# An encoder block on one Trainium2 core: a unit's row gathers start with block 0's first head, and block 1's taps, the taps of blocks 2-3 and the output gate are laid out anew beside them

## The chip, the core and the metric

The kernel runs on one core of one Trainium2 chip. The core's engines run side by side and meet at semaphores: TensorE (PE) multiplies matrices out of the on-chip memory into eight banks, VectorE (DVE) and ScalarE (ACT) work on tiles, GpSimd (POOL) issues the indirect gathers, SyncE (SP) the weight loads. 16 DMA engines carry all transfers. The metric is device time in microseconds (us), lower is better; everything is 32-bit.

## The reference

512 tokens of width 2048 go through a gated mixer and a layer of many small experts:

```python
proj = h @ w_in[l]
q, k, v, og, gkf, gkb, glu, ga, gb = jnp.split(proj, offsets, axis=-1)
...
o = (o * jax.nn.silu(og.reshape(B, S, GLA_HEADS, GLA_DV))).reshape(B, S, GLA_VAL_WIDTH)
y_a = o @ gla_w_o[l]
u = a_in * jax.nn.sigmoid(a_gate)
u = lax.conv_general_dilated(u, conv_w[l][:, None, :], ...)  # 31 taps, each channel alone
u = jax.nn.silu(_layernorm(u, conv_ln_g[l], conv_ln_b[l]))
y_b = u @ conv_w_pw2[l]
merged = jax.nn.sigmoid(ga) * y_a + jax.nn.sigmoid(gb) * y_b
x = x + merged @ w_out[l]
...
# experts: 8 heads; per token and head 16 of 16384 rows, found by two searches among 128 keys
s = jnp.einsum('thcd,hcnd->thcn', q, keys)
s_top, i_top = lax.top_k(s, PEER_TOPK)
...
u = jnp.take(u_tab, idx, axis=0)
act = jax.nn.gelu(jnp.einsum('thkd,td->thk', u, hb))
w = (gate * act)
return jnp.einsum('thk,thkd->td', w, jnp.take(v_tab, idx, axis=0))
```

## The kernel before

The tokens lie in four blocks of 128. The attention part (four heads, all blocks) and block 0's own mixer come first. Then comes the expert layer, which needs a row of 8 KB from `u_tab` and one from `v_tab` for each token, head and choice: 32 **units** (block and head) of 16 **steps**, and in each step 128 rows of either table, 2.1 MB in all. Everything that blocks 1 to 3 still need of the mixer is laid beside the steps of blocks 0 and 1 (steps 0 to 255).

A step on DVE is `add_row` for the step two before (x2 += w * v row, L1311), then `dot` (the u row times the token, summed, L1301), then `beside(s)`, which holds the work of other blocks, and, from unit 7 on, a part of the next unit's search. POOL has two row slots for u and four for v, so it gathers the u row of step s+2 as soon as `dot` of step s is done. ACT makes `expert` (gelu and gate) of each step and then its own `beside(s)`. PE has no steps: it runs through its slabs in the order of the code and waits for banks that DVE or ACT must free, and for weights.

Weights come as **slabs** of 2 MB (256 columns). The ring `wring` has two slots, and SP loads slab n when slab n-2 has been used (`hold(sp, w_used, ...)` in `load`). `project` is one projection of 128 channels over a span of tokens (16 matmuls), `tiles` two of them in one bank.

Beside block 0's steps blocks 1 to 3 get, by the tables at the head of the file (numbers are steps):

- `TURN_AT`: eight turns. In each PE makes the two GLU slabs of two channel tiles over 384 tokens (`glu1`), DVE takes them (`glu1_take`) and then makes 31 taps for each tile over 384 tokens (`conv1`, L1338), spread over the turn's steps. `u_keep` carries the 15 columns at the border to block 0.
- in turns 0 to 3 also two slabs of the output gate each (`og1_scale`, 384 tokens), in turns 4 to 7 two pairs of gate A and W_o for block 1 (`ma1_merge`).
- behind them gate B's eight slabs (`mb1_gate`), the layer norm of the taps over 384 tokens (`ln1`), the pointwise projection (`mb1_merge` at `PW_AT`), the output projection (`RES1_AT`), the norm (`NORM1_AT`) and the eight query heads of block 1, one every second step from 105.
- from step 130 (`M2_AT`) gate A, gate B and the rest for blocks 2-3.

Before the first step, block 0's eight query heads are searched: `topk_parts(0, PH, PH, ...)` makes each head's halves and pairs as its scores come, and then the places, keys and softmax of all eight in one batch (2048 wide). After that, `idx_ready` lets POOL start.

A semaphore wait blocks everything behind it on its engine: this is how a matmul that comes late holds ACT or DVE, and so the gathers.

## Time and profile before

| | before |
|---|---|
| time, median of 3 runs | 4772.74 us (4771.23 to 4778.17) |
| the profiled execution | 4765.59 us, its span 4763.9 us |
| PE busy | 3783.1 us (79%) |
| DVE busy | 2743.7 us (58%) |
| ACT busy | 873.1 us (18%) |
| GpSimd busy | 1339.6 us (28%) |
| DMA | 1530.72 MB, mean 321 GB/s; 1073.81 MB of them gathers |
| first row product, of step 0 | 1303.89 us |
| row product of step 54 | 1798.38 us |
| row product of step 120 | 2379.74 us |
| mean granted TensorE clock | 0.926 |

The shares are means over stages with different limits, so the stretches of the unit loop have to be read one by one. A matmul over 384 columns is a different amount of work from one over 128, and the same line has both; go by the shapes.

### The profile page before, as it was taken

The page shows a single profiled execution, that of the slowest core. Times are in us where ns is not written, and L with a number is a line of the kernel's source. Part 1 is how long each engine was busy: PE and PEld are TensorE (multiplying, and loading weights), DVE is VectorE, ACT ScalarE, POOL GpSimd, SP SyncE. Part 2 cuts the span into 40 slices and gives each one's busy share as a digit, 9 for nine tenths or more (in the row PEclk, how much of TensorE's full clock was granted, in tenths as well). Part 3 has the DMA queues.
Part 4 walks back from the last instruction along what each step waited for, and adds up shares of the span by engine and source line. Part 5 has one row for each costly group of instructions (what it writes and reads, how often), then busy time and mean ns, then how long its engine had stood idle before and what let it go on. Part 6 is the DMA issues. An engine that isn't in the chain of part 4 may idle for free. (4 is left out here: it accounts for less than half of the span.)

```text
span 4763.9 us, 44159 instructions
## 1 busy us (share of the span) xinstructions
PE 3783.1 (79%) x15280; PEld 2399.6 (50%) x15280; DVE 2743.7 (58%) x3996; ACT 873.1 (18%) x2035; POOL 1339.6 (28%) x1038
## 2 busy tenths in 40 slices
PE   6999999999999999766679798510788876777776
PEld 3444469996755576762668685310334432223232
DVE  1332249000599987866677777778665565455444
ACT  1322220100111111241111111111111211212111
POOL 0000000000022221323454444455333333344443
PEclk9999999999999999888889899755899999999999
DMA  2111126677588888999999999999999999999998
GB/s 102 54 70 53 53 106 264 251 273 277 212 336 352 346 363 329 414 407 407 418 388 426 396 426 418 380 360 341 359 372 367 378 357 372 383 420 421 415 417 367
DMA packets 194520, 1530.72 MB, mean 321 GB/s; under 512 B 24279, under 2 KB 30551, under 8 KB 30809
## 3 DMA queue, kind: packets, MB, share of 16 engines
q0 software_dynamic: 147456, 1073.81, 56.3%
q1 hardware_dynamic: 45232, 444.87, 23.6%
q10 hardware_dynamic: 1740, 10.91, 0.6%
q8 instruction: 46, 0.75, 0.1%
q14 instruction: 46, 0.38, 0.0%
HBM read 1525.32 MB, written 4.19 MB: 321 GB/s over the span
## 5 line engine op out<-in xcount | busy, mean ns | idle before, releaser
L582 POOL DMA_INDIRECT arena_c<-in_peer_u,arena_c x384 | 539.4, 1405 | 2904.3 <-DVE arena_c L1301 1563.2
L1301 DVE SCALAR_TENSOR_TENSOR arena_c<-arena_c 128x2048 f32<-128x2048 f32 x384 | 878.8, 2289 | 590.8 <-DMA arena_c<-in_peer_u,arena_c 584.6
L1624 PE MATMUL bank<-arena_h,wring 128*128 128x384 f32 (+3 forms) x3200 | 887.9, 440 | 25.6 <-ACT arena_h L727 9.0
L586 POOL DMA_INDIRECT arena_c<-in_peer_v,arena_c x512 | 643.4, 1257 | 423.5 <-DVE arena_h L1528 171.7
L1728 PE MATMUL bank<-arena_h,wring 128*128 128x128 f32 (+2 forms) x4608 | 660.6, 305 | 100.0 <-DVE arena_h L1380 52.5
L1624 PEld LDWEIGHTS bank<-arena_h,wring 128*128 128x128 f32 x3200 | 542.8, 197 | 367.1 <-issue 160.3
L1728 PEld LDWEIGHTS bank<-arena_h,wring 128*128 128x128 f32 x4608 | 617.0, 193 | 146.1 <-issue 81.8
L1936 PE MATMUL bank<-arena_c,arena_h 128*128 128x512 f32 x1024 | 504.8, 641 | 170.9 <-ACT arena_h L886 150.6
L1970 PE MATMUL bank<-arena_c 128*128 128x512 f32 x1024 | 485.4, 623 | 173.2 <-ACT arena_c L930 162.7
L1311 DVE SCALAR_TENSOR_TENSOR arena_o<-arena_c,arena_o 128x2048 f32<-128x2048 f32 x256 | 600.7, 2346 | 7.1 <-ACT arena_c L765 4.6
L763 ACT ACTIVATE arena_c<-arena_c 128x1 f32<-128x1 f32 x384 | 77.9, 203 | 2206.1 <-DVE arena_c L1301 2206.0
L1528 DVE SCALAR_TENSOR_TENSOR arena_h<-arena_h,arena_c 128x2048 f32<-128x2048 f32 x128 | 292.8, 2292 | 298.1 <-DMA arena_h<-in_peer_u,arena_c 296.9
L1970 PEld LDWEIGHTS bank<-arena_c 128*128 128x128 f32 x1024 | 193.6, 197 | 465.0 <-ACT arena_c L930 246.4
L1936 PEld LDWEIGHTS bank<-arena_c,arena_h 128*128 128x128 f32 x1024 | 200.0, 204 | 446.6 <-issue 262.8
L1728 PE MATMUL bank<-arena_c,wring 128*128 128x128 f32 (+1 forms) x1536 | 238.6, 318 | 48.4 <-ACT arena_c L704 28.9
L1338 DVE SCALAR_TENSOR_TENSOR arena_c<-arena_c,cols 128x384 f32<-128x384 f32 x480 | 259.6, 608 | 0.0
L1728 PEld LDWEIGHTS bank<-arena_c,wring 128*128 128x128 f32 x1536 | 219.7, 198 | 67.3 <-issue 41.0
L1728 PE MATMUL bank<-arena_o,wring 128*128 128x128 f32 (+1 forms) x1536 | 236.9, 317 | 17.1 <-DMA wring<-in_gla_w_o 15.3
L1728 PEld LDWEIGHTS bank<-arena_o,wring 128*128 128x128 f32 x1536 | 217.9, 196 | 36.1 <-DMA wring<-in_gla_w_o 18.0
L1811 PE MATMUL bank<-arena_c 128*128 (+1 forms) x128 | 25.1, 339 | 261.3 <-ACT arena_c L734 258.7
L1649 PE MATMUL bank<-wring,arena_h 128*128 128x512 f32 x512 | 221.9, 594 | 0.3
L1786 PE MATMUL bank<-wring,arena_h 128*128 128x512 f32 x384 | 178.7, 624 | 39.1 <-DMA wring<-in_w_out 25.0
(214 smaller groups left out, 2558.8 us busy)
## 6 DMA issues: line engine op xcount, KB each, us to landing
wring<-in_w_in SPq DMA_DIRECT2D x112, 2048.0 KB, 8.2
wring<-in_gla_w_o SPq DMA_DIRECT2D x24, 2048.0 KB, 9.9
wring<-in_conv_w_pw SPq DMA_DIRECT2D x24, 2048.0 KB, 11.1
wring<-in_w_out SPq DMA_DIRECT2D x24, 2048.0 KB, 13.5
wring<-in_peer_w_q SPq DMA_DIRECT2D x24, 2048.0 KB, 11.0
arena_c<-in_peer_v,arena_c POOLq DMA_INDIRECT x512, 11.4
arena_c<-in_peer_u,arena_c POOLq DMA_INDIRECT x384, 8.4
arena_c<-in_x SPq DMA_DIRECT2D x4, 1024.0 KB, 12.6
```

Of the source, the lines that this page charges most:

```text
L582: pool.indirect_dma_start(out=u_rows[s], out_offset=None, in_=u_tab[0], in_offset=at)\
L586: pool.indirect_dma_start(out=v_rows[s], out_offset=None, in_=v_tab[0], in_offset=at)\
L1301: V.scalar_tensor_tensor(row, row, 1.0, block_of(h2, b), ALU.mult, ALU.mult, accum_out=act_u[:, k:k + 1]).then_inc(u_used, 1)
L1311: V.scalar_tensor_tensor(block_of(x2, b), by_tile(v_row[s]), act_w[:, k:k + 1], block_of(x2, b), ALU.mult, ALU.add).then_inc(v_used, 1)
L1338: ins = V.scalar_tensor_tensor(dst, upad1[:, m, r:r + T1], tap, dst, ALU.mult, ALU.add)
L1528: V.scalar_tensor_tensor(row, row, 1.0, block_of(h2, b), ALU.mult, ALU.mult, accum_out=act_u2[:, m, k:k + 1]).then_inc(u2_used, 1)
L1624: last = M(ps[bank][:, 0:hi - lo], w_slot(slot)[:, k, m * P:m * P + P], act_in[:, k, lo:hi], start=k == 0, stop=k == KT - 1)
L1649: last = M(by_half(ps[b][:]), hT[:, kk, b * P:b * P + P], w_slot_half(s)[:, :, k, :], start=kk == 0, stop=kk == KT - 1)
L1728: last = M(ps[bank][:, m * w:(m + 1) * w], w_slot(slot)[:, k, m * P:m * P + P], act_in[:, k, lo:hi], start=k == 0, stop=k == KT - 1)
L1786: last = M(by_half(ps[bank0 + g * nb + b][:]), lhs(kk, b), w_slot_half(s)[:, :, k, :], start=kk == 0, stop=kk == KT - 1)
L1936: last = M(ps[4 + q][:], diag1[:, k % VS, :], v_row[k % VS][:, q * 512:q * 512 + 512], start=k == 0, stop=k == TOP - 1)
L1970: last = M(ps[4 * m + q][:], diag[:, s, :], v2_row[s][:, q * 512:q * 512 + 512], start=k == 0, stop=k == TOP - 1)
```

## The change

It rearranges the work up to step 127; from step 128 on the order is the same.

- **Start.** Block 0's heads are searched one by one (`topk_0`). The index of head 0 is handed to POOL as soon as it is there; head 1 follows, and heads 2 to 7 are searched beside steps 0 to 5. ACT takes the queries of heads 4 to 7 beside steps 0 and 1.
- **Turns.** They start at step 8 and are 6 or 7 steps long. `glu1` makes the two GLU slabs over 384 tokens and one gate B slab over 128. DVE makes block 1's taps alone (128 columns). The GLU values of blocks 2-3 are put raw into `cv`, and the 15 border columns are kept.
- **Fill.** Blocks 2-3's taps (256 columns) are made from these by `fill`, 63 pieces for each of 8 pairs of tiles (one for two copies, 62 taps), spread by the table `FILL` over steps 53 to 104.
- **Output gate.** All eight slabs come behind the turns, one in three steps from 58; PE starts them only when ACT has taken all of gate B (`pair["mb1"]["sig"]`).
- **Norms.** Block 1 (128 columns) at steps 62 to 68, blocks 2-3 (256 columns, `ln2`) at 115 to 131; PE makes the latter's sums between the queries and the slabs of blocks 2-3.
- **Then** gate A with W_o, one pair in each of steps 81 to 88; the pointwise merges two a step from 91; residuals at 96, 97, 99, 100; block 1's queries one a step from 105.
- Buffers move to make room, and some semaphores are merged (`cv_done`, `mg_done`, `passed`, `out1`).

```diff
-TURN_AT = (0, 10, 20, 30, 40, 47, 54, 61, 68)
-OG_AT = (4, 7)
-IT_AT = (2, 4)
...
+TURN_AT = (8, 15, 21, 28, 34, 41, 47, 54, 60)
+GB_LATER = 3
+OG_AT = tuple(range(58, 82, 3))
+XC1_AT, RSTD1_AT, RECIP1_AT, SCALE1_AT = 62, 65, 66, 67
+IT_AT = tuple(range(81, 89))
...
+FILL = ((53, 0), (78, 70), (86, 250), (95, 420), (104, 8 * 63))
+XC2_AT, RSTD2_AT, RECIP2_AT, SCALE2_AT = 115, 121, 122, 123
...
+            for h in range(2):
+                queries0(h)
+                exponentials(h, 1, work_0)
+            queries0(2)
+            queries0(3)
...
+                if s == 0:
+                    queries0(4)
+                    exponentials(2, 1, work_0)
+                    queries0(5)
+                if s == 1:
+                    queries0(6)
+                    exponentials(3, 1, work_0)
+                    queries0(7)
+                if 2 <= s < 6:
+                    exponentials(s + 2, 1, work_0)
...
-            find, softmax = topk_parts(0, PH, PH, lambda c, b: s_0[:, c, b, :], work_0, lambda a: a[:, 0:PH, :])
-            all_of(find)
-            softmax()
...
+                    chain.mark(V.tensor_tensor(upad1[:, m, PAD:PAD + GL], ps[2 + m][:, 0:GL], sig1[:, m, 0:GL], ALU.mult))
+                    V.tensor_tensor(cv[:, 2 * j + m, 2 * P:T], ps[2 + m][:, P:T1], sig1[:, m, P:T1], ALU.mult)\
                         .then_inc(p["use"], 1)
...
+                if s < PH - 2:
+                    find, softmax = topk_0(s + 2)
+                    all_of(find)
+                    softmax()
...
-                if 0 <= s - QUERY1_AT < 2 * PH and (s - QUERY1_AT) % 2 == 0:
-                    h = (s - QUERY1_AT) // 2
+                if 0 <= s - QUERY1_AT < PH:
+                    h = s - QUERY1_AT
...
+            for h in range(2):
+                find, softmax = topk_0(h)
+                all_of(find)
+                if h == 0:
+                    V.tensor_copy(idx_cur[:, 0, :], idx_all[:, 0, :]).then_inc(idx_ready, 1)
+                softmax()
...
+                slab_ready(first + 2, i, per)
+                pe.wait_ge(pair["mb1"]["sig"], i * 2 + (m0 + 1))
+                tiles(slot, hT, 4 + m0, P, 2 * P, pair["mb1"]["gate"])
                 slab_used()
...
+            pe.wait_ge(pair["mb1"]["sig"], 2 + 8)
+            og1_slab(0)
+            og1_slab(1)
+            pe.wait_ge(pair["glu1"]["use"], 2 + KT)
+            pe.wait_ge(cv_done, 2 * KT)
+            ln_mean(ln1, P, 2 * P)
+            og1_slab(2)
+            for t in range(KT):
+                pe.wait_ge(ln1["sq"], t // 2 + 1)
+                M(ps[1][:, 0:P], ones_d[:], sqr1[:, t // 2 % 3, t % 2, :], start=t == 0, stop=t == KT - 1)\
+                    .then_inc(ln1["sq_used"], 1)
+            for n in range(3, 8):
+                og1_slab(n)
             pe.wait_ge(og1["used"], 4 + KT)
```

On DVE, between two row additions (L1311, L1313) beside gate A's merges. Before, step 44:

```order
L1311 SCALAR_TENSOR_TENSOR arena_o<-arena_c,arena_o 128x16x128
L1301 SCALAR_TENSOR_TENSOR arena_c<-arena_c 128x2048
L1357 TENSOR_TENSOR arena_h<-bank,arena_c 128x2x128
L1338 SCALAR_TENSOR_TENSOR arena_c<-arena_c,cols 128x384 x9
L1311 SCALAR_TENSOR_TENSOR arena_o<-arena_c,arena_o 128x16x128
```

The same engine in the changed program, step 82, which also holds a merge of gate A:

```order
L1313 SCALAR_TENSOR_TENSOR arena_o<-arena_c,arena_o 128x16x128
L1303 SCALAR_TENSOR_TENSOR arena_c<-arena_c 128x2048
L1376 TENSOR_TENSOR arena_h<-bank,arena_c 128x2x128
L1327 SCALAR_TENSOR_TENSOR arena_c<-arena_c,cols 128x256 x23
L1313 SCALAR_TENSOR_TENSOR arena_o<-arena_c,arena_o 128x16x128
```

The nine taps of 384 columns beside a merge have become 23 of 256 columns, and a merge now comes in every step.

On ACT, at the end of block 0's queries. Before, behind the loop over the heads (L745 is the exponential of all eight, L763 and L765 are step 0's expert):

```order
L745 ACT_TABLE_LOAD
L745 ACTIVATE arena_c<-arena_c 128x128
L772 ACT_TABLE_LOAD
L772 ACTIVATE arena_c<-bank0 128x384
L772 ACTIVATE arena_c<-bank1 128x384
L763 ACT_TABLE_LOAD
L763 ACTIVATE arena_c<-arena_c 128x1
L765 ACTIVATE arena_c<-arena_c,gate_all 128x1
```

In the changed program, from step 0's expert (L751, L753) over head 4's queries (L717) and scores (L722) to head 2's exponential (L728):

```order
L751 ACT_TABLE_LOAD
L751 ACTIVATE arena_c<-arena_c 128x1
L753 ACTIVATE arena_c<-arena_c,gate_all 128x1
L717 ACTIVATE arena_c<-bank0 128x128
L717 ACTIVATE arena_c<-bank1 128x128
L722 ACTIVATE arena_c<-bank2 128x128
L722 ACTIVATE arena_c<-bank3 128x128
L728 ACT_TABLE_LOAD
L728 ACTIVATE arena_c<-arena_c 128x16
```

Head 2's exponential now stands behind head 4's queries, which wait for PE.

On PE, behind block 1's last GLU slab. Before: gate A's last two pairs, gate B, and the norm's sums over 384 columns (L1884, L1889):

```order
L1728 MATMUL bank<-arena_h,wring 128x128 x32
L1728 MATMUL bank<-arena_o,wring 128x128 x32
L1728 MATMUL bank<-arena_h,wring 128x128 x32
L1728 MATMUL bank<-arena_o,wring 128x128 x32
L1728 MATMUL bank<-arena_h,wring 128x128 x128
L1884 MATMUL bank<-arena_c,ones_d 128x384 x16
L1889 MATMUL bank<-arena_c,ones_d 128x384 x4
```

In the changed program, between block 1's last query head and the slabs of blocks 2-3:

```order
L1859 MATMUL bank<-arena_c 128x128
L1955 REGISTER_ALU
L1955 COMPARE_AND_BRANCH
L1921 MATMUL bank<-arena_c,ones_d 128x256 x16
L1965 MATMUL bank<-arena_c,ones_d 128x256 x16
```

The sums over blocks 2-3 have moved from before the pointwise projection to behind the queries.

## Rows read from the trace of the kernel before

**Rows 1.** The page's 40 slices: busy tenths of the DMA engines.
```profile
DMA  2111126677588888999999999999999999999998
```
**Rows 2.** Stretches: length, busy us (x) of PE, PEld, DVE, ACT, POOL, PEclk, DMA share, GB/s.
```profile
2063.00:2147.00 84.00, 67.13 (x513) 65.64 (x514) 47.95 (x49) 28.18 (x45) 19.03 (x19) 0.89 1.00 411
2147.00:2233.00 86.00, 63.56 (x128) 26.01 (x126) 41.56 (x32) 11.79 (x26) 27.19 (x18) 0.88 1.01 422
2258.00:2375.00 117.00, 76.78 (x544) 74.82 (x544) 82.04 (x87) 14.99 (x64) 56.01 (x33) 0.82 1.00 415
1892.00:1973.00 81.00, 64.49 (x512) 63.03 (x512) 71.73 (x90) 20.09 (x33) 20.09 (x16) 0.89 0.97 398
1640.00:1980.00 340.00, 303.40 (x1731) 237.68 (x1730) 284.41 (x373) 65.14 (x116) 73.64 (x64) 0.96 0.90 363
1303.00:1640.00 337.00, 331.67 (x1017) 191.65 (x1016) 312.16 (x388) 57.12 (x122) 88.65 (x78) 1.00 0.89 345
...
885.00:1130.00 245.00, 230.70 (x1995) 224.91 (x1995) 9.35 (x22) 15.14 (x31) 0.00 (x0) 1.00 0.71 269
```
**Rows 3.** DVE's timeline, start and us: from the first scores to the first step.
```profile
1214.44 0.49 DVE L1190 MAX8 arena_c<-arena_c 128x8 f32<-128x128 f32 x2 [15.45 <-ACT arena_c L739]
...
1295.61 0.17 DVE L1455 COPY arena_c<-idx_all 128x16 uint32<-128x16 uint32 x1
1303.89 2.29 DVE L1301 SCALAR_TENSOR_TENSOR arena_c<-arena_c 128x2048 f32<-128x2048 f32 x1 [8.11 <-DMA arena_c<-in_peer_u,arena_c]
...
1314.74 0.56 DVE L1322 TENSOR_TENSOR arena_c<-bank,arena_c 128x384 f32<-128x384 f32 x1 [7.99 <-PE bank L1624]
```
**Rows 4.** DVE's timeline: a step without a wait, and block 0's taps.
```profile
1497.98 2.28 DVE L1301 SCALAR_TENSOR_TENSOR arena_c<-arena_c 128x2048 f32<-128x2048 f32 x1
...
1500.19 3.26 DVE L1338 SCALAR_TENSOR_TENSOR arena_c<-arena_c,cols 128x384 f32<-128x384 f32 x6
1503.37 2.34 DVE L1311 SCALAR_TENSOR_TENSOR arena_o<-arena_c,arena_o 128x2048 f32<-128x2048 f32 x1
1505.63 2.28 DVE L1301 SCALAR_TENSOR_TENSOR arena_c<-arena_c 128x2048 f32<-128x2048 f32 x1
...
799.71 12.43 DVE L1112 SCALAR_TENSOR_TENSOR arena_c<-arena_c,cols 128x128 f32 x47
```
**Rows 5.** DVE's timeline: the halves and the pairs of one head alone (unit 7).
```profile
2326.89 0.48 DVE L1190 MAX8 arena_c<-arena_c 128x8 f32<-128x128 f32 x2
...
2330.30 2.35 DVE L1311 SCALAR_TENSOR_TENSOR arena_o<-arena_c,arena_o 128x2048 f32<-128x2048 f32 x1
...
2336.72 0.42 DVE L1220 TENSOR_TENSOR arena_c<-arena_c 128x256 f32<-128x256 f32 x1
...
2339.68 2.35 DVE L1311 SCALAR_TENSOR_TENSOR arena_o<-arena_c,arena_o 128x2048 f32<-128x2048 f32 x1
```
**Rows 6.** PE's timeline: GLU pair, a pointwise slab, first query, first slab of blocks 2-3.
```profile
1272.79 41.92 PE L1624 MATMUL bank<-arena_h,wring 128*128 128x384 f32 x128 [0.46 <-ACT arena_c L739]
...
2063.80 9.18 PE L1728 MATMUL bank<-arena_c,wring 128*128 128x128 f32 x64 [28.95 <-ACT arena_c L704]
...
2073.33 7.38 PE L1728 MATMUL bank<-arena_c,wring 128*128 128x128 f32 x64 [0.36 <-issue]
...
2257.95 9.37 PE L1624 MATMUL bank<-arena_h,wring 128*128 128x128 f32 x64 [3.49 <-ACT arena_h L727]
...
2375.05 15.60 PE L1728 MATMUL bank<-arena_h,wring 128*128 128x256 f32 x64 [0.67 <-ACT arena_c L739]
```
**Rows 7.** DVE's timeline: the row products of steps 54 and 120.
```profile
1798.38 2.29 DVE L1301 SCALAR_TENSOR_TENSOR arena_c<-arena_c 128x2048 f32<-128x2048 f32 x1
...
2379.74 2.29 DVE L1301 SCALAR_TENSOR_TENSOR arena_c<-arena_c 128x2048 f32<-128x2048 f32 x1 [5.25 <-DMA arena_c<-in_peer_u,arena_c]
```
**Rows 8.** Weight loads of 1303 to 1640, then of 1990 to 2400: median us to landing.
```profile
wring<-in_w_in SPq DMA_DIRECT2D x16, 2048.0 KB, 10.8
...
wring<-in_w_out SPq DMA_DIRECT2D x8, 2048.0 KB, 13.8
```

More of the change, by code:

```diff
@@ L60 @@
 SB_GLU1 = SB_WQ0 + PH
[L61 to L65 removed]
+SB_OG1 = SB_GLU1 + 24
+SB_MA1 = SB_OG1 + 8
+SB_PW1 = SB_MA1 + 16
 SB_OUT1 = SB_PW1 + 8
@@ L1312, in add_row, with taps @@
                                        ALU.mult, ALU.add).then_inc(v_used, 1)
+            def taps(j, first, end, src, lo, hi, done):
+                for n in range(first, end):
+                    r, m = n // 2, n % 2
+                    dst = cv[:, 2 * j + m, lo:hi]
+                    tap = cols[:, 2 * j + m, R_CW + r:R_CW + r + 1]
+                    if r == 0:
+                        ins = V.tensor_scalar(dst, src[:, m, 0:hi - lo], tap, cols[:, 2 * j + m, R_CB:R_CB + 1],
+                                              ALU.mult, ALU.add)
+                    else:
+                        chain.wait(but=1)
+                        ins = V.scalar_tensor_tensor(dst, src[:, m, r:r + hi - lo], tap, dst, ALU.mult, ALU.add)
+                    if r < TAPS - 1:
+                        chain.mark(ins)
+                    else:
+                        ins.then_inc(done, 1)
+                        chain.wait()
             def glu1_take(j):
@@ L1398, in beside @@
+                if s in OG_AT:
+                    og1_scale(OG_AT.index(s))
+                if s == XC1_AT:
                     dve.wait_ge(ln1["sum"], 1)
-                    dve.wait_ge(cv1_done, KT)
-                    mean = ps[0][:, 0:T1].unsqueeze(1).broadcast_to([P, 2, T1])
-                    for g in range(2 * (s - XC_AT), 2 * (s - XC_AT) + 2):
-                        dst = cv[:, 2 * g:2 * g + 2, P:T]
-                        V.tensor_tensor(dst, dst, mean, ALU.subtract).then_inc(ln1["xc"], 1)
@@ new lines, in beside @@
+                if s <= FILL[-1][0]:
+                    fill(filled(s - 1), filled(s))
+                if 0 <= s - XC2_AT < 4:
+                    dve.wait_ge(ln2["sum"], 1)
+                    dve.wait_ge(cv_done, 3 * KT)
+                    mean = ps[0][:, 0:T2].unsqueeze(1).broadcast_to([P, 2, T2])
+                    for g in range(2 * (s - XC2_AT), 2 * (s - XC2_AT) + 2):
+                        dst = cv[:, 2 * g:2 * g + 2, 2 * P:T]
+                        V.tensor_tensor(dst, dst, mean, ALU.subtract).then_inc(ln2["xc"], 1)
@@ L1829, in _, with glu1 @@
             pe.wait_ge(s_ev, 2 * PH)
-            def glu1(first, i, per, before, j):
+            def glu1(first, i, per, m0):
                 p = pair["glu1"]
+                slot = first % 2
                 slab_ready(first, i, per)
                 for m in range(2):
-                    pe.wait_ge(p["use"], j * 2 + (2 * before + m + 1))
-                    project(0, m, hT, m, p["gate"], P, T)
+                    pe.wait_ge(p["use"], i * 4 + (2 * m0 + m + 1))
+                    project(slot, m, hT, m, p["gate"], P, T)
                 slab_used()
@@ L1852, in ma1 @@
                 slab_used()
[L1854 to L1862 removed]
+            with pe.Fori(0, PH // 2) as i:
+                for m in range(2):
+                    glu1(SB_GLU1 + 3 * m, i, 6, m)
@@ new lines, in og1_slab, with ln_mean @@
+            def og1_slab(n):
+                slab_ready(SB_OG1 + n)
+                for m in range(2):
+                    pe.wait_ge(og1["used"], 2 * n + m + 1)
+                    project(n % 2, m, hT, 4 + 2 * (n % 2) + m, og1["mm"], P, T)
+                slab_used()
+            def ln_mean(ln, lo, hi):
+                for t in range(KT):
+                    last = M(ps[0][:, 0:hi - lo], ones_d[:], cv[:, t, lo:hi], start=t == 0, stop=t == KT - 1)
+                last.then_inc(ln["sum"], 1)
@@ L1863, in _ @@
             pe.wait_ge(og1["used"], 4 + KT)
[L1864 removed]
+            with pe.Fori(0, PH // 2) as i:
                 for a in range(2):
[L1866 to L1876 removed]
@@ L1878, in _ @@
-            pe.wait_ge(pair["ma1"]["use"], 2 + 8)
-            for n in range(4):
-                mb1_gate(n)
-            pe.wait_ge(pair["glu1"]["use"], 2 + KT)
-            pe.wait_ge(cv1_done, KT)
-            for t in range(KT):
-                last = M(ps[0][:, 0:T1], ones_d[:], cv[:, t, P:T], start=t == 0, stop=t == KT - 1)
-            last.then_inc(ln1["sum"], 1)
-            for n in range(4):
-                for t in range(4 * n, 4 * n + 4):
-                    pe.wait_ge(ln1["sq"], t + 1)
-                    M(ps[1][:, 0:T1], ones_d[:], sqr1[:, t % 2, :], start=t == 0, stop=t == KT - 1)\
-                        .then_inc(ln1["sq_used"], 1)
-                mb1_gate(4 + n)
+                    ma1(SB_MA1 + 2 * a, i, 4, a, i * 2 + (a + 1))
```

347 lines of the change are left out of this document (160 added, 187 removed).

## The prediction

> **What bounds the kernel now.** Start with the page's slices [rows 1]: from slice 17 (1906 us) on the 16 DMA engines are nine tenths busy or more, but for the last slice; in the five before, eight tenths. The stretches with their sums [rows 2] say what is busy instead. At 1303 to 1640 us TensorE (PE) is busy for 332 of 337 us and DVE for 312, the DMA moves 345 GB/s; at 1640 to 1980 it is 303 and 284 of 340 at 363 GB/s; from 2063 on it is DMA alone, 411 to 422 GB/s, with PE and DVE half idle. So two regimes stand one behind the other in the unit loop: first PE and DVE together, then DMA. All that the change touches lies between the first score (1214 us) and the first slab of blocks 2-3 (PE at 2375.05 us, just before the step of 2379.74 us) [rows 3, 6, 7]. Behind that point the program is the same, and the DMA is full, so what is gained or lost there is carried to the end one for one. I therefore follow PE and DVE to that point.
>
> **The prices.** A step's row product and row addition follow each other at 2.21 and 2.26 us, and six 384-wide taps between them take 3.18, so a step is 4.47 us and a tap 0.53 [rows 4]. 47 taps of 128 columns take 12.43 us, 0.264 each [rows 4]. A 256-wide tap is not in the trace: its bounds are 0.264 and 0.53, and the line through both gives 0.397, which I take. A split tap thus costs 0.264 + 0.397 - 0.53 = 0.13 us more, and 496 of them 65 us of DVE: both parts pay what does not depend on the columns. The Trainium skill (VectorE: DVE Perf Modes, on the TRN2 errata) speaks against such a split: each instruction pays its fixed latency, and it gives 58 cycles plus the columns at 0.96 GHz, while noting that this row is too low. By its row the split would cost an estimated 30 us in place of 65; the 128-wide row here is above it (0.264 against an estimated 0.19 us), so the trace decides.
> One head's search alone: halves 3.41 us (2326.89 to 2330.30), pairs 2.96 (2336.72 to 2339.68), six 256-wide ones for the keys at the 0.45 of such a row, 2.7, and ten small ones of 0.07 to 0.2 [rows 5], together 10.4 us.
> PE: a 384-wide slab (two projections) is 41.92 / 2 = 20.95 us, a 128-wide one 7.4 (7.38 in [rows 6]). The ring has two slots, so a slab's load starts when the slab two before it is used, and short slabs go at (7.4 + load) / 2 each (my reading of the code). Without gathers 32 of them take 245 us, 7.7 each; with gathers beside them eight took 81 us from 1892 and eight 84 us from 2063, 10.1 to 10.5 each [rows 2]. Load times are 10.8 us beside gathers and up to 13.8 for a half-slab at full DMA [rows 8].
>
> **The start.** Removed: the wait of 8.11 us for the first row and the batch's tail [rows 3]. Now: head 0's index is ready 10.3 us after its scores, at 1225, and the first row lands about 8.3 us later (1295.61 to 1303.89), at 1234. DVE has head 1 done at 1236 and makes dot 0. But beside steps 0 to 5 it makes six more searches: 8 x 4.47 + 6 x 10.4 = 98 us, and ScalarE stands between: it holds the queries of heads 4 to 7 in front of the exponentials, so steps 0 and 1 end only with PE's heads 4 and 6, about 15 us lost. Step 8, where block 1's first GLU pair is taken, comes at 1344. PE finished that pair at 1320 (its search phase ends 5 us later than before), and waits. Before, it was taken at 1315 in step 0 [rows 3]. So eight steps are won and 29 us of PE lost.
>
> **The turns (steps 8 to 54).** PE now makes two 384-wide slabs and one 128-wide one: 42 + 7.4. The next pair's first slab starts to load when the second long slab is used, so it comes after the load (10 us, by the row of 10.8) and not after 7.4: 52.3 a turn. DVE needs 6.5 steps x 4.47 + 62 x 0.264 + 1.9 for the take = 47.4. PE ends the turns: first two by DVE (to 1440), five by PE, last take at 1701. Before, step 54 was at 1798 [rows 7].
>
> **Output gate (steps 54 to 79).** PE may not start before ScalarE has taken the last B gate, three steps after the take (1731): 22 us idle. Then 8 slabs x 20.95, one mean and one square sum (4 and 5 us): 1910 at step 79. DVE needs some 5.8 us a step (4.47, 2.8 wide taps, a third of the gate's two products of 0.5) and PE gives 7, so DVE waits in step 58 (11 us), 62, 64 and then every third.
>
> **Gate A with W_o (steps 79 to 88).** 16 short slabs. DVE has 22.5 wide taps a step: 4.47 + 8.9 + 0.4 = 13.8. PE: with gathers at half their pace I take 8.7 a slab (bounds 7.7 and 10.1), 17.4 a pair, one pair a step: the ring ends it, last merge 2050.
>
> **Pointwise (88 to 94).** PE waits for the merges of step 91, DVE has 19 taps a step (12.0 us): last merge 2137, where before it was about 2146, just ahead of the projection [rows 2].
>
> **Output projection (to step 100).** Before 86 us [rows 2]; with fewer gathers beside it I take loads of 11.5 in place of 13.8 [rows 8]: 73, to 2211. Then one residual, three steps with nine taps each, the norm and the transposes: queries start at 2252 (before 2257.95, [rows 6]).
>
> **Queries.** Before 117 us for eight heads, 14.6 each, since a head went with two steps; now one step a head. At 4.2 MB per head and step and 415 to 422 GB/s: 10 us, less two slabs that are there: 77, to 2329.
>
> **Blocks 2-3's norm.** New on PE's path: mean (7 us), then the squares of steps 116 to 119, which wait for seven DVE steps of 5.5 to 6.5 us: PE starts blocks 2-3's slabs at 2374 in place of 2375, step 120 at 2377 in place of 2380.
>
> **Sum.** 41 us of the queries, 13 of the projection and the 97 us by which the steps had run ahead at step 54 are given back in gate A, in the taps beside it, and in 45 us of the new norm. Shift -1 to -3: the profiled execution's 4765.6 us would be 4763, and the median of the three timed runs, 7 us above it, 4770.
>
> **Rivals.** All three engines are near their ends here. DVE's own work from step 8 to 120 is 112 x 4.47 + 496 x 0.661 + some 67 of merges and norms = 896 us in my 1030, and DMA has 112 x 2.1 MB and 70 slabs of 2.1 MB, 382 MB, 371 GB/s.
> Faster: the loads are quick where the gathers pause at a take or a merge. With the 7.7 of the stretch without gathers: turns -15, gate A -15, projection -11, queries -11, about -50: 4720. For it speaks that DMA at 415 GB/s would need 920 us only, and DVE 896; against it the 10.8 of a stretch that was not full.
> Slower: the two-slot ring keeps the full pace's price of 10.1 a slab: gate A + 22, turns + 8, and PE partly at 1.2 GHz after each wait (9.18 us for a slab after 28.95 us idle, in place of 7.38 [rows 6], in a stretch of granted clock 0.89 [rows 2]) in the pointwise, query and norm parts, + 8: 4808. It decides from 9.3 us a slab on. For it speaks that each of these parts lies beside gathers.
> The DMA pages' limit. Rows show 422 GB/s over 86 us [rows 2]; the Trainium skill (DMA: Bandwidth & Descriptors, where 436 GB/s comes from) says that HBM to SBUF binds near 358 GB/s per core. Were it so, 382 MB would need an estimated 1067 us, + 37: 4807. The trace disagrees, 2 in 100.
> The change does not do what it says: the first searches beside steps 0 to 5 could run without ScalarE's hold, -11, or hold all six steps, + 25. This only moves the cases above.
>
> **How the numbers follow.** The sum holds within 20 us: 0.42, of it a third faster, half the same. Quick loads (4700 to 4750): 0.30. Slow ring (4785 to 4830): 0.26, the limit of HBM 0.02. The measurement tells 0.2%, 9.5 us, from no change: faster 0.43, same 0.24, slower 0.33. The range of 8 in 10, 4712 to 4815, takes in most of both rivals; the likeliest case alone has 4750 to 4790.
>
> **What would show it.** First gather near 1226 us; first take near 1344, with PE idle some 17 us before the next 384-wide slab; turns of 52 us with a gap of 2 to 3 us before each pair; a PE gap of 20 us before the first output-gate slab; short slabs in gate A at 8.7 us each; queries at 10 us a head; first 256-wide slab of blocks 2-3 at 2374. If the turns or the gate A pairs are off by more than 2 us each, or wide taps cost more than 0.42 us, the forecast falls.

## The result

The changed kernel takes 4810.26 us (median of 7 runs, 4795.67 to 4813.93), the kernel before 4778.98 beside it (7 runs, 4771.23 to 4791.29): a ratio of 1.0054, 95% interval 1.0036 to 1.0071. Measured again later it was 4808.08 against 4773.66 us, 1.0073 (1.0054 to 1.0092). It is slower by 25 to 35 us. The forecast was 4770 us, 3 us less than the 4772.74 of the kernel before that it started from, so the sign was missed; the time lies in the range, at the place of the rival "slow ring" (4808). The two executions that were profiled lie 45 us apart (4810.88 and 4765.59), the medians 31, so the two traces side by side show the loss some 14 us too large.

### The profile page after: what moved, and what is told of

It is laid out like the page before. It is cut to its first block and busy times, and to the rows that moved or that the text cites. A ratio compares the mean times of both kernels' runs of the same rounds, so it can differ in the third digit from the quotient of the medians.

```text
span 4809.1 us, 44984 instructions
## 1 busy us (share of the span) xinstructions
PE 3795.9 (79%) x15344; PEld 2409.2 (50%) x15344; DVE 2831.0 (59%) x4650; ACT 893.5 (19%) x2064; POOL 1473.1 (31%) x1038
## 5 line engine op out<-in xcount | busy, mean ns | idle before, releaser
L565 POOL DMA_INDIRECT arena_c<-in_peer_u,arena_c x384 | 518.6, 1350 | 2815.3 <-DVE arena_c L1303 1528.2
L1672 PE MATMUL bank<-arena_h,wring 128*128 128x384 f32 (+3 forms) x3200 | 896.4, 443 | 89.6 <-DMA wring<-in_w_in 20.9
L569 POOL DMA_INDIRECT arena_c<-in_peer_v,arena_c x512 | 800.4, 1563 | 424.1 <-DVE arena_h L1576 171.2
L1313 DVE SCALAR_TENSOR_TENSOR arena_o<-arena_c,arena_o 128x2048 f32<-128x2048 f32 x256 | 600.7, 2347 | 2.7
L751 ACT ACTIVATE arena_c<-arena_c 128x1 f32<-128x1 f32 x384 | 77.8, 203 | 2054.9 <-DVE arena_c L1303 2054.8
L1327 DVE SCALAR_TENSOR_TENSOR arena_c<-arena_c,cols 128x128 f32<-128x128 f32 (+1 forms) x960 | 324.6, 410 | 0.0
```

Source lines behind the costliest of these rows:

```text
L565: pool.indirect_dma_start(out=u_rows[s], out_offset=None, in_=u_tab[0], in_offset=at)\
L569: pool.indirect_dma_start(out=v_rows[s], out_offset=None, in_=v_tab[0], in_offset=at)\
L1313: V.scalar_tensor_tensor(block_of(x2, b), by_tile(v_row[s]), act_w[:, k:k + 1], block_of(x2, b), ALU.mult, ALU.add).then_inc(v_used, 1)
L1327: ins = V.scalar_tensor_tensor(dst, src[:, m, r:r + hi - lo], tap, dst, ALU.mult, ALU.add)
L1672: last = M(ps[bank][:, 0:hi - lo], w_slot(slot)[:, k, m * P:m * P + P], act_in[:, k, lo:hi], start=k == 0, stop=k == KT - 1)
```

## The profile after

**Where the time went.** The prediction said that all of the difference arises between the first scores and step 120, and is then carried on one for one. These are that stretch and all behind it, for the kernel before and then the changed one (length, busy us of PE, PEld, DVE, ACT, POOL, granted clock, DMA share, GB/s):

```profile
1199.00:2379.70 1180.70, 996.98 (x4911) 724.68 (x4912) 918.07 (x1211) 239.32 (x502) 317.82 (x244) 0.93 0.89 359
2379.70:4760.00 2380.30, 1684.83 (x4947) 944.89 (x4945) 1481.86 (x1880) 428.45 (x1201) 1019.35 (x780) 0.89 0.97 388
```
```profile
1206.00:2424.60 1218.60, 999.91 (x4955) 727.24 (x4956) 998.35 (x1858) 227.63 (x495) 456.34 (x243) 0.91 0.88 348
2424.60:4805.00 2380.40, 1691.59 (x4966) 949.63 (x4965) 1488.80 (x1891) 460.53 (x1237) 1014.41 (x782) 0.89 0.97 388
```

The second rows are 2380.30 and 2380.40 us long: behind step 120 nothing changed. Ahead of the stretch the changed kernel was 7 us later (1206 against 1199), in block 0's own mixer, whose slabs stand in the same order in both. That is not scatter alone: the first scores come at 1214.4 and 1215.2 us in the two traces that run the old code there (before and e5), and at 1217.9 to 1222.3 in all eleven of the changed kernel and its edits. At 885 us they are still together; from there to 1130 us PE was busy for 230.70 us before [rows 2], and after for

```profile
885.00:1130.00 245.00, 226.54 (x1943) 220.70 (x1943) 9.35 (x22) 15.13 (x31) 0.00 (x0) 0.99 0.70 261
```

(226.0 to 227.7 us in all eleven), with waits for the loads of w_in of 7.2 us in place of 2.0. So 3 to 8 us of the loss lie ahead of all that the forecast looked at; what in the change makes them was not tested. The stretch itself is 37.9 us longer (29.7 in the trace of c0, the changed kernel measured again). PE is busy for 3 us more, so nearly all of it is idle PE: 183.7 us before, 218.7 now. DVE's 80 us more stand beside that and needn't be its cause. And the transfers, which do the same work in both, fell from 359 to 348 GB/s.

**Which waits.** Groups of PE's instructions in the same stretch, the large ones (busy us, mean ns, idle time before them and what ended it), first of the kernel before:

```profile
L1624 PE MATMUL bank<-arena_h,wring 128*128 128x384 f32 (+1 forms) x2560 | 632.0, 410 | 15.3 <-issue 5.2 <-ACT arena_h L727 4.4 <-DMA wring<-in_w_in 4.3
L1728 PE MATMUL bank<-arena_h,wring 128*128 128x128 f32 (+1 forms) x1039 | 125.9, 283 | 17.3 <-DMA wring<-in_w_in 13.1 <-issue 2.9 <-ACT arena_c L739 0.7
L1728 PE MATMUL bank<-arena_c,wring 128*128 128x128 f32 x512 | 66.7, 297 | 43.2 <-ACT arena_c L704 28.9 <-DMA wring<-in_conv_w_pw 13.6 <-issue 0.7
L1728 PE MATMUL bank<-arena_o,wring 128*128 128x128 f32 x512 | 65.0, 293 | 14.7 <-DMA wring<-in_gla_w_o 14.5
L1811 PE MATMUL bank<-arena_c 128*128 x64 | 14.0, 352 | 42.6 <-ACT arena_c L734 42.6
L1580 PE MATMUL bank<-ident,arena_c 128*128 128x128 f32 x32 | 7.3, 424 | 25.0 <-DVE arena_c L1175 25.0
```
and of the changed one:
```profile
L1672 PE MATMUL bank<-arena_h,wring 128*128 128x384 f32 (+1 forms) x2560 | 639.7, 413 | 79.2 <-DMA wring<-in_w_in 20.9 <-ACT arena_c L777 20.4 <-DVE arena_c L1345 18.5
L1776 PE MATMUL bank<-arena_h,wring 128*128 128x128 f32 x1024 | 122.8, 282 | 16.7 <-DMA wring<-in_w_in 11.1 <-issue 2.7 <-DVE arena_h L1376 1.5
L1776 PE MATMUL bank<-arena_c,wring 128*128 128x128 f32 x512 | 65.1, 293 | 30.0 <-DVE arena_c L1387 22.6 <-DMA wring<-in_conv_w_pw 6.2 <-DVE arena_h L1376 0.8
L1776 PE MATMUL bank<-arena_o,wring 128*128 128x128 f32 x512 | 64.1, 290 | 14.0 <-DMA wring<-in_gla_w_o 13.9
L1965 PE MATMUL bank<-arena_c,ones_d 128*128 128x256 f32 x27 | 12.7, 642 | 23.0 <-ACT arena_c L829 23.0
L1859 PE MATMUL bank<-arena_c 128*128 x64 | 12.0, 313 | 8.6 <-ACT arena_c L717 8.6
L1628 PE MATMUL bank<-ident,arena_c 128*128 128x128 f32 x32 | 7.3, 424 | 34.9 <-DVE arena_c L1178 34.9
```

The 384-wide slabs, which hardly waited before (15.3 us), wait for 79.2 now: for loads in the turns (20.9), for ScalarE's last B gate ahead of the output gate (20.4), for DVE to reach step 8 (18.5). The scores wait 34 us less (42.6 to 8.6), since a head goes with one step; the pointwise slabs 13 less; blocks 2-3's squares wait 23.0 us and the norm's transposes 10 more. The short slabs of gates A and B and of W_o wait for their loads no longer than before: 27.6 us then (13.1 and 14.5), 25.0 now. So gate A's loads are a miss of the forecast, as shown below, and not what the change lost against the kernel before; that lies mostly in the long slabs.

**The parts.** The stretches of after that answer to [rows 2]: start, turns, output gate, gate A, pointwise, projection, queries, blocks 2-3's norm.

```profile
1226.00:1354.00 128.00, 102.47 (x628) 82.20 (x626) 108.44 (x335) 32.89 (x69) 22.84 (x20) 0.94 0.80 316
1354.00:1727.00 373.00, 347.63 (x1280) 217.57 (x1280) 332.06 (x623) 68.10 (x143) 240.89 (x95) 0.97 0.94 373
1755.00:1935.00 180.00, 175.92 (x576) 104.49 (x576) 142.23 (x178) 53.83 (x104) 82.49 (x43) 0.99 0.86 336
1936.00:2091.00 155.00, 127.62 (x1024) 124.59 (x1024) 121.65 (x236) 29.12 (x45) 19.47 (x20) 0.92 0.91 359
2091.00:2187.00 96.00, 65.08 (x512) 63.70 (x512) 79.05 (x153) 2.98 (x12) 11.76 (x12) 0.84 0.82 313
2187.00:2265.00 78.00, 62.57 (x128) 25.73 (x128) 62.10 (x107) 2.98 (x12) 12.94 (x12) 0.91 0.96 394
2299.00:2382.00 83.00, 69.39 (x544) 66.76 (x544) 48.09 (x51) 12.03 (x50) 31.83 (x19) 0.93 0.95 394
2382.00:2427.00 45.00, 21.86 (x65) 15.02 (x66) 40.24 (x50) 9.33 (x32) 16.33 (x12) 0.70 0.91 350
```

Only the output gate has one engine busy throughout (PE, 175.92 of 180 us). No part reaches the 411 to 422 GB/s that the kernel before had from 2063 us on [rows 2]. The page's slices, where [rows 1] had nine tenths from slice 17 on, show a break in it, in slice 18:

```profile
DMA  2111136677789989989999999998999999999998
```

**Steps.** Rows of DVE's timeline that answer to [rows 3] and [rows 7]: the first scores, the first row product, and those of steps 8, 54, 120 and 128.

```profile
1221.90 0.49 DVE L1193 MAX8 arena_c<-arena_c 128x8 f32<-128x128 f32 x2 [15.74 <-ACT arena_c L722]
...
1242.97 2.29 DVE L1303 SCALAR_TENSOR_TENSOR arena_c<-arena_c 128x2048 f32<-128x2048 f32 x1
...
1352.22 2.29 DVE L1303 SCALAR_TENSOR_TENSOR arena_c<-arena_c 128x2048 f32<-128x2048 f32 x1 [0.91 <-DMA arena_c<-in_peer_u,arena_c]
...
1719.32 2.29 DVE L1303 SCALAR_TENSOR_TENSOR arena_c<-arena_c 128x2048 f32<-128x2048 f32 x1 [1.25 <-DMA arena_c<-in_peer_u,arena_c]
...
2424.57 2.28 DVE L1303 SCALAR_TENSOR_TENSOR arena_c<-arena_c 128x2048 f32<-128x2048 f32 x1
...
2483.14 2.29 DVE L1303 SCALAR_TENSOR_TENSOR arena_c<-arena_c 128x2048 f32<-128x2048 f32 x1 [4.74 <-DMA arena_c<-in_peer_u,arena_c]
```

At step 54 the steps are 79 us ahead of before (1719.3 against 1798.4), at step 80, by the same rows, 103 (1946.7 against 2049.8); at step 88 it is 37, at step 96 they are 20 behind (2208.4 against 2188.6), at step 120 they are 45. So 123 us are lost in 16 steps: gate A and the pointwise part take two slabs to a step, 16.4 us a step, where before a step took 8.7.

## The experiments

The theories as the expectations name them. **R**, later **P**: a part ends with PE, the load of its next slab (two slots) and the engine that PE hands to; the time is the sum of that chain. **V**: DVE's added work is the loss. **S**: what counts of the early start is gathers made early. **G** came up after the first four runs: what counts is PE's chain and also how many steps lie beside it, since a step that doesn't fit there is made later at its full price. Every time has the kernel before beside it on its chip: 4779.68 us for the first four, 4773.66 for c0, e6, e7 and e9, 4781.62 for e5, e8 and e10. "Against the change" is by the ratios to before for the first four, by the medians of one set for the rest.

### e1_few_taps: blocks 2-3's taps left out

```diff
-                        taps(j, at - 1, at, upad2, 2 * P, T, cv_done)
+                        if at <= 2 or at > 60:
+                            taps(j, at - 1, at, upad2, 2 * P, T, cv_done)
```


> The changed kernel with 56 pieces of each 62 taps of blocks 2-3 left out (its output for them is another one), 464 wide taps of 0.397 us, 184 us of DVE, in steps 53 to 104. Theory R (from step 8 on PE and the load of its next slab end each part, DVE waits): gate A's 16 slabs stay at 150 to 155 us, the pointwise part loses PE's wait of 21 us, the rest little, so 25 to 45 us less than the changed kernel (profiled 4809). Theory V (DVE's added work, 65 us of split taps and 62 us of searches beside steps, sets the time): DVE's parts shrink by its work, 100 us or more less, gate A's part under 125 us.

4779.44 us (8 runs), ratio 0.9997 (0.9985 to 1.0009): 27 to 36 us less than the change (by its first and second ratio), within R's bounds, far from V's. That is as much as the whole loss: without 184 us of DVE's taps the kernel is level with the one before. Gate A beside it:

```profile
1925.00:2080.00 155.00, 132.26 (x1031) 128.10 (x1029) 52.25 (x58) 30.32 (x46) 23.76 (x21) 0.91 0.92 366
```

DVE is busy for 52.25 us in place of 121.65, and the part is as long: 1928.43 to 2079.6, 151 us against 155. Its 16 slabs, not DVE, end it. The gain came mostly behind it, where PE waits for DVE: the third pointwise slab waited 7.99 us, not 21.16, the norm's transposes 17.7, not 27.8. V falls for gate A and stands for these places.

### e2_gate_banks: the first output-gate slab into free banks

PE need not wait for ScalarE's last B gate before that slab. The banks change in the programs of ScalarE and DVE too.
```diff
-                    project(n % 2, m, hT, 4 + 2 * (n % 2) + m, og1["mm"], P, T)
+                    project(n % 2, m, hT, 6 - 2 * (n % 2) + m, og1["mm"], P, T)
...
-            pe.wait_ge(pair["mb1"]["sig"], 2 + 8)
             og1_slab(0)
+            pe.wait_ge(pair["mb1"]["sig"], 2 + 8)
             og1_slab(1)
```


> The changed kernel, but the output gate's first slab goes to the banks that gate B does not use, so PE need not wait for ScalarE's last gate B: PE's gap of 20.4 us before the output gate should go. Theory R: PE is what later parts wait for, so 12 to 20 us less than the changed kernel (about 1.001 to 1.003 of the kernel before in place of 1.0054). Theory V: the steps do not move, 0 to 5 us.

4790.77 us (10 runs), ratio 1.0025 (1.0014 to 1.0036): 14 to 23 us less than the change. The wait of 20.43 us is now 3.16, for a load, and the slab starts 18 us earlier:

```profile
1736.95 22.60 PE L1672 MATMUL bank<-arena_h,wring 128*128 128x384 f32 x64 [3.16 <-DMA wring<-in_w_in]
```

A handover of 20 us that the forecast had right was simply a cost of the change, and it could be had without.

### e3_half_loads: half of each slab in gate A not loaded

```diff
-            pair_loads(SB_MA1, w_in, WGA, w_o, 0)
+            with sp.Fori(0, KT // 2) as i:
+                load(SB_MA1, i, 2, slot_all(0)[:, 0:SLAB // 2], slab(w_in, i + WGA)[:, 0:SLAB // 2])
+                load(SB_MA1 + 1, i, 2, slot_all(1)[:, 0:SLAB // 2], slab(w_o, i)[:, 0:SLAB // 2])
```


> The changed kernel, but each of the 16 slabs of block 1's gate A and W_o loads only its first half (the other half of the slot is what was there, so block 1's values are others). Theory R (the two-slot ring's load sets 9.7 us a slab there): the part from 1936 to 2091, 155 us, falls to 120 to 130, and the whole by 20 to 30 us. Theory V: DVE's 13.9 us a step set that part, it stays above 145 and the whole within 8 us.

4781.57 us (10 runs), ratio 1.0009 (1.0000 to 1.0019): 21 to 31 us less. The part and two of its slabs, then two of the same part in the changed kernel:

```profile
1925.00:2052.00 127.00, 118.69 (x1025) 115.54 (x1024) 122.12 (x237) 30.33 (x46) 20.52 (x21) 1.00 0.80 300
1943.39 7.41 PE L1778 MATMUL bank<-arena_h,wring 128*128 128x128 f32 x64 [0.50 <-issue]
1951.25 7.41 PE L1778 MATMUL bank<-arena_o,wring 128*128 128x128 f32 x64 [0.46 <-DMA wring<-in_gla_w_o]
```
```profile
1957.35 10.03 PE L1776 MATMUL bank<-arena_h,wring 128*128 128x128 f32 x64 [5.32 <-DMA wring<-in_w_in]
...
2042.71 10.02 PE L1776 MATMUL bank<-arena_o,wring 128*128 128x128 f32 x64 [4.56 <-DMA wring<-in_gla_w_o]
```

155 us became 127, 7.9 a slab, with all of DVE's work in place (122.12 of it). This shows the load as what ends gate A, in two ways: the wait of up to 5 us, and a slab that takes 10.03 us in place of 7.41 behind such a wait, at a granted clock of 0.92 in the part against 1.00 without waits. The second is 9 of the 28 us (127.62 less 118.69).

### e4_late_start: all eight heads searched before the first gather

```diff
-            for h in range(2):
+            for h in range(8):
```
This stands in DVE's and in ScalarE's program, and the searches beside steps 0 to 5 go. ScalarE then makes a head's exponential behind the next head's queries, and head 0's index is handed over last.

> The changed kernel with its early start undone: all eight heads are searched one by one before the first gather, none beside a step. First row product about 1318 us in place of 1243. Theory R: step 8's take needs only eight bare steps of 4.5 to 5.5 us, so it comes at 1363 in place of 1354 and the whole is 8 to 15 us longer. Rival S (the gathers done early are what a start is worth): the 75 us by which the first product comes later are carried on, 50 us or more longer.

4827.7 us (4 runs), ratio 1.0106 (1.0087 to 1.0125), 16 to 25 us more than the change: between R's 8 to 15 and S's 50. The first and the ninth row product, and PE's second GLU pair:

```profile
1313.84 2.29 DVE L1293 SCALAR_TENSOR_TENSOR arena_c<-arena_c 128x2048 f32<-128x2048 f32 x1 [9.84 <-DMA arena_c<-in_peer_u,arena_c]
...
1368.22 2.29 DVE L1293 SCALAR_TENSOR_TENSOR arena_c<-arena_c 128x2048 f32<-128x2048 f32 x1 [1.90 <-DMA arena_c<-in_peer_u,arena_c]
```
```profile
1371.21 4.21 PE L1657 MATMUL bank<-arena_h,wring 128*128 128x384 f32 x6 [39.32 <-DVE arena_c L1335]
```

The first product is 71 us later, the ninth only 16 (1368.2 against 1352.2): with the searches out of the way eight steps take 54 us and not 109. So the early start is worth 16 us where the take stands at step 8, for the searches have to be made anyway. It was not the loss.

### e5_split_before: the kernel before with its taps split, nothing moved

Each tap of 384 columns becomes one of 128 and one of 256.
```diff
...
-                        ins = V.scalar_tensor_tensor(dst, upad1[:, m, r:r + T1], tap, dst, ALU.mult, ALU.add)
+                        chain.mark(V.scalar_tensor_tensor(near, upad1[:, m, r:r + P], tap, near, ALU.mult, ALU.add))
+                        chain.wait(but=3 if r < TAPS - 1 or m == 0 else 2)
+                        ins = V.scalar_tensor_tensor(far, upad1[:, m, P + r:r + T1], tap, far, ALU.mult, ALU.add)
```


> The kernel before with one thing of the change alone: each of its 480 taps of 384 columns is made as two, 128 and 256 columns wide, in the same place. That is the price of narrower taps without any move: in the traces 960 narrow taps took 324.6 us and 480 wide ones 259.6, so DVE has 65 us more to do, 8.1 us in each of the eight turns. Theory V (DVE's added work is the loss): +65 us against the kernel before, 4837 to 4845. Theory G (the added work costs only where DVE ends a turn; in the trace of before PE ended turns 4 to 7 and waited about 4.5 us for DVE in the first four): +20 to +45 us. If it costs less than 10 us, DVE's added work is out as a cause in both kernels.

4797.96 us (10 runs), ratio 1.003 (1.0015 to 1.0044): 14 to 16 us, below both expectations. The takes of the GLU pairs in 1340 to 2000 us tell why, in the kernel before and then here:

```profile
L1322 DVE TENSOR_TENSOR arena_c<-bank,arena_c 128x384 f32<-128x384 f32 x14 | 7.8, 555 | 57.9 <-PE bank L1624 57.9
```
```profile
L1322 DVE TENSOR_TENSOR arena_c<-bank,arena_c 128x384 f32<-128x384 f32 x14 | 7.4, 560 | 11.2 <-PE bank L1629 11.2
```

DVE used to wait 57.9 us for PE in these turns and now waits 11.2. So 47 of some 65 us more of work went into idle time, and the rest shows in the time. I had taken DVE to end the first four turns, with nothing to spare; its waits for PE say that it had 58 us to spare in all. The split alone, in its old place, costs 15 us.

### c0_change_again, e6_pointwise_early, e7_taps_away

> The changed kernel once more, unedited, beside the other three on the same chip: it is what they are compared with. Both theories: the ratio of the first measurement, 1.0054 (1.0036 to 1.0071), so 4800 to 4814 us. If it falls outside, the distances of the edits measured so far (about -27, -14, -21 and +25 us) have to be read anew.

4808.08 us (4 runs), 1.0073 (1.0054 to 1.0092), as expected; its trace passes step 128 at 2472.3 us, 11 us earlier than the one above, which is how far two executions can differ.

e6: pointwise merges and all behind them two steps earlier.
```diff
-PW_AT = 91
-GAIN1_AT = 95
-RES1_AT = (96, 97, 99, 100)
-NORM1_AT = 101
-QUERY1_AT = 105
+PW_AT = 89
+GAIN1_AT = 93
+RES1_AT = (94, 95, 97, 98)
+NORM1_AT = 99
+QUERY1_AT = 103
```


> The changed kernel with everything from the pointwise merges on (merges, residual, norm, queries of block 1) beginning two steps earlier (merges at steps 89 to 92 instead of 91 to 94). In the trace of the changed kernel PE waited 21.16 us for the third pointwise slab until DVE reached step 91. Theory P (the chain of PE, its slabs and the two engines it hands to is all that counts): the wait goes, PE is done with the pointwise part about 15 us earlier and everything behind it too, -10 to -18 us against the changed kernel. Theory G (row gathers and slabs share transfers that run at 394 to 420 GB/s from the projection on, and each step that is not made beside a slow part is made later at 7.3 us): the two steps that no longer fit beside the unit come back behind it, 2 x 7.3 = 14.6 us, which eats the gain: -5 to +3 us.

4809.18 us (4 runs), 1.0062 (1.0044 to 1.008): 1 us more than c0 by the medians, 5 less by the ratios, both as G said. With intervals of 9 us to either side the times alone don't shut out the near end of P's 10 to 18; the trace speaks against P. PE's wait of 21 us did go. Then the projection, with the steps beside it, took 94 us in place of 78, and at the end PE waited for the squares of blocks 2-3, which hang on step 115:

```profile
2168.00:2262.00 94.00, 63.73 (x128) 26.16 (x128) 76.94 (x136) 4.39 (x15) 13.94 (x13) 0.87 0.87 346
```
```profile
2406.81 3.86 PE L1965 MATMUL bank<-arena_c,ones_d 128*128 128x256 f32 x8 [30.58 <-ACT arena_c L829]
```

A wait that is taken from PE by asking for its result at an earlier step is not gained if the steps themselves come no sooner.

e7: the same wait attacked from the other side. 55 taps (by the table, 57 less 2) leave steps 89 to 91, most of them for the output-gate part, and no step moves.
```diff
-FILL = ((53, 0), (78, 70), (86, 250), (95, 420), (104, 8 * 63))
+FILL = ((53, 0), (60, 20), (78, 130), (88, 346), (91, 348), (95, 440), (104, 8 * 63))
```


> The changed kernel with the taps of blocks 2 and 3 spread otherwise: 57 of them leave steps 89 to 91 and go to the output-gate part (steps 60 to 78, where DVE was busy for 142 of 180 us). No step or slab moves in the order. DVE then comes to the first pointwise merge about 20 us earlier (4.6 instead of 12.2 us of work in each of three steps). Theory P: PE's wait of 21.16 us goes, -12 to -20 us. Theory G: the same, since here the steps come earlier with PE: -12 to -20 us. A theory that DVE's total work sets the time (nothing of it is taken away here): 0 to -3 us.

4798.87 us (4 runs), 1.0049 (1.0032 to 1.0066): 9 us less than c0 by the medians, 11 by the ratios, where both theories had 12 to 20; four runs of each don't tell 9 from 12. The wait fell from 21.16 to 9.33 us, but the taps went where DVE had less room than I took: PE waits there now (the wait was 1.43 us).

```profile
1931.85 3.56 PE L1776 MATMUL bank<-arena_h,wring 128*128 128x128 f32 x15 [7.33 <-DVE arena_o L1369]
```

### e8_banks_taps, e9_more_steps, e10_one_more

e8 is e2's and e7's edits together. e9 has in addition 11 steps in place of 8 beside gate A (the loads of x and of the gain, the residual and the taps' table move along):
```diff
-IT_AT = tuple(range(81, 89))
...
-PW_AT = 91
...
-NORM1_AT = 101
-QUERY1_AT = 105
+IT_AT = (81, 82, 84, 85, 87, 88, 90, 91)
...
+PW_AT = 94
...
+NORM1_AT = 104
+QUERY1_AT = 108
...
-XC2_AT, RSTD2_AT, RECIP2_AT, SCALE2_AT = 115, 121, 122, 123
+XC2_AT, RSTD2_AT, RECIP2_AT, SCALE2_AT = 117, 123, 124, 125
```


> The changed kernel with two of the three edits of e9_more_steps: the free banks for the first output-gate slab, and the 57 taps moved out of the steps at the head of the pointwise part. Steps stand as in the changed kernel. It tells apart what the third edit (three steps more beside the slabs of gate A) is worth. Theory P: the third edit is worth nothing, so this one is at e9's time, 4758 to 4768 us. Theory G: it is worth three steps of 7.3 us, 22 us, so this one is at 4780 to 4790 us; the sum of the two edits alone, -14 and -9 us from 4808, gives 4785.

> The changed kernel with three edits: the first output-gate slab goes to two free banks (as in e2_gate_banks, measured at 4790.77 us); 57 taps leave the steps at the head of the pointwise part (as in e7_taps_away); and the 8 merges of block 1's gate A are spread over 11 steps instead of 8 (steps 81 to 91), with all that comes after three steps later, and the second normalisation of blocks 2-3 two steps later. Theory P: only the first two edits count, -14 - 16 = -30 us against the changed kernel, 4778 to 4785 us: level with the kernel before. Theory G: three more pairs of gathers lie beside slabs that leave room (359 GB/s there, against 410 behind), and three steps of 7.3 us less remain behind: -14 - 16 - 22 = -52 us, 4752 to 4765 us, faster than both kernels.

e8: 4787.85 us (10 runs), 1.0014 (1.0001 to 1.0026). e9: 4762.7 us (7 runs), 0.9974 (0.9958 to 0.999), **faster than both kernels**. Both as G said and P did not: three more steps beside the slabs are worth 0.0040 of the ratio, 19 us, or 25 by the medians of the two sets; G had 22. 140 us of gate A in e9, where the changed kernel moved 359 GB/s in 155 us with 10 pairs of rows:

```profile
1930.00:2070.00 140.00, 116.17 (x964) 113.32 (x963) 126.46 (x232) 28.53 (x46) 24.00 (x24) 0.96 0.97 400
```

It moves 400 GB/s, and the granted clock is 0.96. The part got no longer for its additional gathers: from its first slab to the first pointwise one it took 150 us in e8 (from 1920.2) and 149 in e9 (from 1918.4). DVE's taps per step fell from some 22 to 16, so the steps fit where transfers and PE had room. Step 128 comes at 2423.4 us, against 2472.3 in c0 and 2437.1 before. One thing moves with the third edit: the squares of blocks 2-3 are asked for at step 117, two steps later and not three, and PE's waits for them fell from 20.8 us in e8 to 14.3. So up to 6 of the 19 us may be that and not the steps; no run parts them.

e10 puts one more step beside the pointwise part (merges at steps 94 to 98).


> e9_more_steps with the 8 pointwise merges spread over 5 steps (94 to 98) instead of 4 and all that comes after one step later. Theory G: one step less remains behind the unit, -7 us against e9_more_steps, 4752 to 4760 us, if DVE does not become the one waited for in the pointwise part (68 of 93 us busy there in e9). Theory P: 0 us, or some us slower, since merges then come later than PE has their slabs.

4761.09 us (10 runs), 0.9967 (0.9951 to 0.9982). Against e9 that is 2 us by the medians, 3 by the ratios: the intervals overlap, so it doesn't tell the two apart. Its trace has a reason why not all 7 us came: the third pointwise slab waited 10.3 us for DVE, in e9 6.5. It too is faster than before.

## Why the prediction missed

The parts in order, as forecast and as the profile of after has them:

| part | forecast, us | measured | off |
|---|---|---|---|
| all before the first scores | as before | 7.5 later (1221.90 against 1214.44) | +7.5 |
| to the first take | 1344 | 1354.5 | +3 beside that |
| turns, to step 54's take | 357 | 372 | +15 |
| wait for ScalarE | 30 (of it PE idle 22) | 28 (20.43) | -2 |
| output gate | 179 | 180 | +1 |
| gate A with W_o | 140 | 155 | +15 |
| pointwise | 87 | 95 | +8 |
| projection | 74 | 79 | +5 |
| residual and norm, to the queries | 41 | 35 | -6 |
| queries | 77 | 82 | +5 |
| blocks 2-3's norm | 45 | 45.2 | 0 |
| first slab of blocks 2-3 | 2374 | 2426.97 | +53 |

The rows add up to 51.5; what is left is rounding. They go by one execution; c0's trace is 10 us earlier at step 120. The first take has an error of addition as well: the forecast's own terms (head 1 done at 1236, 98 us of steps and searches, 15 lost) give 1349, not 1344, and with the 7.5 us from ahead that is 2 us from the 1354.5 measured.

**What held.** The order of the parts and where PE stands idle: 18.49 us before the second pair (forecast some 17), 20.43 before the output gate (22). The length of the new norm, 45.2 us (45). Which engine ends each part, but for the first two turns: the forecast had DVE end them, and PE waited there for loads (3.40 and 4.25 us). The price of a 256-wide tap, which no trace had shown: 19 take 7.60 us, 0.400 each, for a forecast of 0.397. That what is lost by step 120 is carried on one for one: 2380.30 against 2380.40 us. And e4's 16 us for the start bear out that most of the eight steps won is paid for by the searches.

**The step that failed** is the price of the load. The prediction put the pairs of turns after a load of 10 us and gate A at 8.7 us a slab, between bounds of 7.7 and 10.1; measured were 9.7 (155 / 16), beyond the 9.3 from which it said that the slow ring decides. The loads landed in 10.9 us (the median beside the first turns), and in gate A in 9.0 and 12.0 by turns:

```profile
wring<-in_w_in SPq DMA_DIRECT2D x7, 2048.0 KB, 9.0
wring<-in_gla_w_o SPq DMA_DIRECT2D x7, 2048.0 KB, 12.0
```

That is 10.5 in the mean. Half the sum of 10.5 and a slab of 7.98 (127.62 / 16) gives 9.2, where half the sum of 10 and 7.4 gives the forecast's 8.7; the other 0.5 has no term in that formula. I had taken 8.7 because gathers go at half their pace there. The rows [rows 2] had 10.1 to 10.5 for eight short slabs beside gathers, at 398 and 411 GB/s, and those were the nearer rows. e3 shows this term for gate A: with half of the bytes the part took 127 us. The turns fail by the same term, as their trace reads; no run took their loads away. PE's gaps before the pairs were 3.40, 4.25, 5.73, 1.29, 1.89 and 4.32 us for a forecast of 2 to 3. Behind the four long ones the pair took 43.5 to 44.9 us in place of 41.9, 9 us in all. The last five turns took 54.6 us each by PE, not 52.3.

```profile
1410.04 43.53 PE L1672 MATMUL bank<-arena_h,wring 128*128 128x384 f32 x128 [3.40 <-DMA wring<-in_w_in]
...
1465.56 23.76 PE L1672 MATMUL bank<-arena_h,wring 128*128 128x384 f32 x64 [4.25 <-DMA wring<-in_w_in]
```

**The rivals.** "Slow ring" was right in mechanism and place. That its 4808 is so near the time measured is luck: it put 22 us on gate A and 8 on the turns, where the trace has 15 and 15, and it had nothing for the 7 us ahead of the first scores or the kernel before's own median, 6 us above the 4772.74 it started from. It had the lower clock behind waits for the pointwise, query and norm parts alone; e3 shows it in gate A too, 9 us, and the turns have as much (granted clock 0.97 there, against 1.00 at 1303 to 1640 us before). "Quick loads" is refuted: no part came at 7.7 us a slab; only with half of the bytes was it 7.9. The limit near 358 GB/s that the Trainium skill states (DMA: Bandwidth & Descriptors, where 436 GB/s comes from) doesn't hold in the changed kernel either, which moved 412 and 420 GB/s over 200 and 270 us. The same page ties that figure, just above, to two cores that share the memory and stream at once; here one core ran:

```profile
2630.00:2830.00 200.00, 167.26 (x755) 143.19 (x754) 142.83 (x145) 41.14 (x81) 97.80 (x55) 0.93 1.00 412
2830.00:3100.00 270.00, 218.13 (x733) 138.22 (x731) 200.83 (x238) 42.99 (x98) 117.77 (x73) 0.92 1.01 420
```

**What the sum lacked.** It weighed only who ends a part. The steps that had run 103 us ahead were spent at two slabs a step in gate A and in the pointwise part. e8 and e9 show that the number of steps beside such a part is a lever of its own, and one that the change left unused. What stays open: what made the 3 to 8 us ahead of the first scores; and how much of a step's 7.3 us behind the unit is transfers and how much is DVE's remaining taps. In e6's projection DVE was busy for 77 of 94 us at 346 GB/s, so there it was not the transfers alone.

## What to carry over

With a weight ring of two slots, price a short slab beside other traffic at half of the sum of its load time and its own time behind a wait, both read from a stretch that has that traffic, as a lower bound (9.2 us where 9.7 were measured), and take a value below the nearest row only if a row shows it. When slow and fast parts stand one behind the other, count how many units of the background work lie beside each part: moving a result's due step forward gains nothing if the units come no sooner, while fitting three more units beside transfers that were at 359 GB/s gained about 19 us here. Before paying for narrower instructions look at what the engine waits for: of 65 us more of DVE's work 47 vanished in its waits.
